# A decoder trunk on one core: token gather with a PSUM bank per feature block, ranks by tile, high halves first

## What is computed

```python
for l in range(DEPTH):
    mix = hybrid_mixer(x, positions, w_in[l], ...)       # 4 latent, 6 forgetting, 6 dilated heads
    x = layer_norm(ALPHA * x + mix, ...)
    xa = memory_cross_attention(x, mem, xattn_w_q[l], xattn_w_kv[l], xattn_w_o[l])   # 4 heads, 256 tokens
    x = layer_norm(ALPHA * x + xa, ...)
    gates = shared_group_router(x, router_w, router_bias)
    x = layer_norm(ALPHA * x + moe_ffn(x, gates, w_gate, w_up, w_down), ...)

def shared_group_router(x, router_w, router_bias):       # 16 experts in 4 groups of 4
    scores = sigmoid(x @ router_w)
    grp = (scores + router_bias).reshape(B, S, 4, 4)
    g_sel = argmax(sum of the two best of each group)
    expert_idx = two best experts inside group g_sel
    w = scores[expert_idx]; w = w / sum(w)
    return one_hot(expert_idx) * w
```

## Time and profile before

| what | value |
|---|---|
| three runs | 843.35, 837.23, 838.66 us |
| median | 838.66 us |
| the profiled execution | 841.01 us |
| its span | 839.4 us |
| mean granted clock of TensorE | 0.988 |
| memory traffic | 177 MB, 211 GB/s over the span |

### The profile page before, as it was taken

The page is one execution under the profiler, slowest core; times in us unless marked ns, Lnnn a source line. Parts: engine busy times, 40 slices in busy tenths (PEclk is TensorE's granted clock), DMA queues, the critical chain, the costliest instruction groups (busy, mean ns, idle before and its releaser), DMA issues.

```text
span 839.4 us, 12175 instructions
## 1 busy us (share of the span) xinstructions
PE 807.6 (96%) x4382; PEld 692.6 (83%) x4382; DVE 631.0 (75%) x1098; ACT 499.9 (60%) x788; POOL 87.1 (10%) x165
## 2 busy tenths in 40 slices
PE   7899999999998999999999999999999999999995
PEld 7899887789876888888899998868998768888884
DVE  4657868785558899999755686787655679999995
ACT  4755554454435788888455654645443557888872
POOL 3148100020000000000020440001000100000001
PEclk9999999999999999999999999999999899999998
DMA  9954433473334799999655543435633339999951
GB/s 284 336 180 167 138 124 127 152 241 114 126 100 126 243 369 366 366 368 377 212 156 168 203 151 109 147 131 172 204 102 124 126 102 313 364 370 364 369 198 51
DMA packets 122095, 177.06 MB, mean 211 GB/s; under 512 B 10177, under 2 KB 90577, under 8 KB 122033
## 3 DMA queue, kind: packets, MB, share of 16 engines
q1 hardware_dynamic: 120048, 169.56, 60.5%
q0 software_dynamic: 1984, 6.70, 2.9%
HBM read 175.18 MB, written 1.05 MB: 210 GB/s over the span
## 4 chain that ended last, share of the span: by engine, by line
PE 81%; DVE 9%; ACT 3%; issue 3%; DMA 2%; POOL 1%; SPq 0%; DVEq 0%; POOLq 0%; ACTq 0%
PE bank L1527 22%; PE bank L1529 22%; PE bank L1528 21%; DVE w_split L506 2%; DMA raw<-in_w_in_dram 2%; PE bank L1670 2%; PE bank L1711 2%; PE bank L1681 1%; DVE xs L1098 1%; PE bank L1702 1%; PE bank L1607 1%; PE bank L1818 1%; DVE xT_lo L1025 1%; PE bank L1659 1%; DVE xs L1146 1%
## 5 line engine op out<-in xcount | busy, mean ns | idle before, releaser
L506 DVE TENSOR_TENSOR w_split<-raw,w_split 128x1024 fp32r<-128x1024 f32 (+3 forms) x336 | 387.5, 1176 | 79.0 <-ACT w_split L501 73.5
L501 ACT ACTIVATE w_split<-raw 128x1024 fp32r<-128x1024 f32 (+3 forms) x336 | 335.7, 1010 | 108.8 <-PE bank L1529 93.9
L1527 PE MATMUL bank<-w_split,xg_hi 128*128 128x512 f32 x256 | 103.8, 406 | 0.0
L1528 PE MATMUL bank<-w_split,xg_hi 128*128 128x512 f32 x256 | 100.6, 393 | 0.0
L1529 PE MATMUL bank<-w_split,xg_lo 128*128 128x512 f32 x256 | 100.6, 393 | 0.0
L1527 PE MATMUL bank<-w_split,xT_hi 128*128 128x384 f32 (+2 forms) x224 | 78.2, 349 | 4.4 <-DVE w_split L506 3.6
L1529 PE MATMUL bank<-w_split,xT_lo 128*128 128x384 f32 (+2 forms) x224 | 76.3, 341 | 0.0
L1528 PE MATMUL bank<-w_split,xT_hi 128*128 128x384 f32 (+2 forms) x224 | 76.2, 340 | 0.0
L618 POOL TENSOR_SCALAR st<-st 128x1 f32<-128x1 f32 x12 | 5.6, 469 | 643.4 <-ACT junk_end L774 336.2
L1529 PEld LDWEIGHTS bank<-w_split,xg_lo 128*128 128x128 f32 x256 | 48.3, 189 | 11.0
L1527 PEld LDWEIGHTS bank<-w_split,xg_hi 128*128 128x128 f32 x256 | 48.5, 189 | 9.1
(11 more groups left out here) (305 smaller groups left out, 1589.7 us busy)
## 6 DMA issues: line engine op xcount, KB each, us to landing
raw<-in_expert_w_gate_dram SPq DMA_DIRECT2D x128, 256.0 KB, 5.4
raw<-in_expert_w_up_dram SPq DMA_DIRECT2D x128, 256.0 KB, 6.7
raw<-in_expert_w_down_dram SPq DMA_DIRECT2D x64, 512.0 KB, 7.3
raw<-in_xattn_w_kv_dram SPq DMA_DIRECT2D x32, 512.0 KB, 3.9
raw<-in_w_in_dram SPq DMA_DIRECT2D x40, 384.0 KB, 3.9
raw<-in_w_mix_out_dram SPq DMA_DIRECT2D x16, 512.0 KB, 3.7
raw<-in_xattn_w_q_dram SPq DMA_DIRECT2D x16, 512.0 KB, 3.5
raw<-in_xattn_w_o_dram SPq DMA_DIRECT2D x16, 512.0 KB, 5.0
```

The source lines that it names most:

```text
L501: nc.scalar.activation(w_hi[:, i % SPL, 0:w], raw[:, i % RAW, 0:w], ACT.Copy).then_inc(hi_ready, 1)
L506: nc.vector.tensor_tensor(w_lo[:, i % SPL, 0:w], raw[:, i % RAW, 0:w], w_hi[:, i % SPL, 0:w].bitcast(F32), ALU.subtract).then_inc(lo_ready, 1)
L1527: nc.tensor.matmul(o, lhs[0], rhs[0], start=first, stop=False, skip_group_check=shared)
L1528: nc.tensor.matmul(o, lhs[0], rhs[1], start=False, stop=False, skip_group_check=shared)
```

## The change

`XG_APART` goes: all eight feature blocks have a bank of their own, blocks 6 and 7 the banks 5 and 4. ScalarE makes eight `xg_hi` and VectorE eight `xg_lo`. The ranks of tile 0 and of tile 1 go to banks 4 and 5, with a signal each; the count of each group goes to bank 5 too, and is compared (`over_full`) ahead of block 6, whose first matmul waits for it. `iota` starts at 1, and the −1 step goes. In the routing two pairs of independent steps wait together. `router_first` moves from ahead of the ranks to behind the last `xg_lo`, two splits move ahead of the first `xg_lo`. The fillers become 6, 3, 11 and 2.

The logits are made by half tiles, high products first, and `XT0c`'s second low half moves behind tile 1's addition and scaling. The logits lie in pair 2. `XQ0`'s first piece is made with its high-half products first (`high_first`); `XT0b` moves to pair 3. `head_qk` of head 10 no longer waits for `s_masked`. The overflow path has a semaphore for each layer, and GpSimd's branch for the case without overflow goes.

```diff
-        ("XT0b", 2, 2, 0), ("XT1b", 2, 2, 2), ("MV1", 0, 2, 1), ("XQ0", 2, 0, 0), ("XQ1", 2, 0, 1),
-        ("XO0", 0, 2, 0), ("XO1", 0, 0, 1), ("XT0c", 2, 2, 0), ("XT1c", 2, 2, 1), ("RT", 1, 0, 0)]
+        ("XT0b", 2, 2, 3), ("XT1b", 2, 2, 2), ("MV1", 0, 2, 1), ("XQ0", 2, 0, 0), ("XQ1", 2, 0, 1),
+        ("XO0", 0, 2, 0), ("XO1", 0, 0, 1), ("XT0c", 2, 2, 0), ("XT1c", 2, 2, 1), ("RT", 1, 0, 2)]
...
-XG_BANKS = (0, 6, 7, 2, 3, 1)
-XG_APART = {6: (6, 7), 7: (2, 3)}
+XG_BANKS = (0, 6, 7, 2, 3, 1, 5, 4)
...
         more, both = (R[i][:, 0:2 * TT * NG].rearrange("p (g i) -> p g i", i=2) for i in (4, 5))
-        step(nc.vector.tensor_tensor(more, first, second, ALU.max))
-        step(nc.vector.tensor_tensor(both, first, second, ALU.add))
         across, within, score = (G4(R[i]) for i in (6, 7, 8))
-        step(nc.vector.tensor_tensor(across, more[:, :, 0], more[:, :, 1], ALU.add))
-        step(nc.vector.tensor_tensor(within, both[:, :, 0], both[:, :, 1], ALU.max))
+        step(nc.vector.tensor_tensor(more, first, second, ALU.max),
+             nc.vector.tensor_tensor(both, first, second, ALU.add))
+        step(nc.vector.tensor_tensor(across, more[:, :, 0], more[:, :, 1], ALU.add),
+             nc.vector.tensor_tensor(within, both[:, :, 0], both[:, :, 1], ALU.max))
         step(nc.vector.tensor_tensor(score, across, within, ALU.max))
...
-    def place_tokens(l):
+    def place_tokens(l, t):
         step = stepper(l)
-        dve.wait_ge(ranked.sem, ranked.at(l, 1))
-        pg = posg[:, :, :].rearrange("p t g -> p (t g)")
-        step(nc.vector.tensor_tensor(pg, bank[4][:, 0:TT * NG], ing, ALU.mult))
-        step(nc.vector.tensor_scalar(pg, pg, -1.0, None, ALU.add))
+        dve.wait_ge(ranked.sem, ranked.at(l, t + 1))
+        step(nc.vector.tensor_tensor(posg[:, t, :], bank[4 + t][:, 0:NG], ing[:, t * NG:(t + 1) * NG], ALU.mult))
...
             .then_inc(sel_ready.sem, 1)
+
+    def low_tokens(l, t):
         dve.wait_ge(xs_a.sem, xs_a.at(l, t + 1))
...
+    def over_full(l):
+        nc.vector.tensor_scalar(fl[:, 0:NG], bank[5][:, NG:2 * NG], P + 0.5, None, ALU.is_gt)\
+            .then_inc(counted_over.sem, 1)
+
     def full_group(l):
-        nc.vector.tensor_scalar(fl[:, 0:NG], bank[4][:, TT * NG:TT * NG + NG], P + 0.5, None, ALU.is_gt)\
-            .then_inc(counted_over.sem, 1)
         dve.wait_ge(counted_over.sem, counted_over.at(l, 1))
-        nc.vector.tensor_tensor(fl[:, NG:2 * NG], fl[:, 0:NG], iota[:, 0:NG], ALU.mult).then_inc(counted_over.sem, 1)
+        nc.vector.scalar_tensor_tensor(fl[:, NG:2 * NG], iota[:, 0:NG], -1.0, fl[:, 0:NG], ALU.add, ALU.mult).then_inc(counted_over.sem, 1)
         dve.wait_ge(counted_over.sem, counted_over.at(l, 2))
...
             split_lo(dve, index[l, "RT", j])
-        turn_x(l, "XT0c", 0)
+        turn_half(l, "XT0c", 0, 0)
         wait_job(l, "XO1")
...
         scale(l, 1, 1)
+        turn_half(l, "XT0c", 0, 1)
         norm_halves(l, 1, 1, x_half)
...
         router_groups(l)
-        router_first(l)
-        place_tokens(l)
+        place_tokens(l, 0)
         choose(l, 0)
+        place_tokens(l, 1)
+        over_full(l)
+        low_tokens(l, 0)
         choose(l, 1)
+        low_tokens(l, 1)
         split_lo(dve, u + 1)
-        for f in range(KC - len(XG_APART)):
+        split_lo(dve, u + 2)
+        for f in range(KC):
             dve.wait_ge(xg_a.sem, xg_a.at(l, f + 1))
...
                 .then_inc(xg_v.sem, 1)
-            if f in (1, 5):
-                split_lo(dve, u + (2 if f == 1 else 3))
+            if f == 3:
+                split_lo(dve, u + 3)
         split_lo(dve, u + 4)
+        router_first(l)
         router_gates(l)
...
+    def high_first(l, name, turned_by):
+
+        open_job(l, name)
+        w_parts = sub_in(index[l, name, 0])
+        for t_ in turned_by:
+            pe.wait_ge(job_a.sem, job_a.at(l, evac_a[job[t_]]))
+        for high in (True, False):
+            if not high:
+                for t_ in turned_by:
+                    ready(l, t_)
+            for kc in range(2):
+                for cb in range(4):
+                    o = banks(name)[cb // 2][:, (cb % 2) * T:(cb % 2 + 1) * T]
+                    hi, lo = (v[:, kc * 512 + cb * P:kc * 512 + (cb + 1) * P] for v in w_parts)
+                    if high:
+                        nc.tensor.matmul(o, hi, xT_hi[:, kc, :], start=kc == 0 and cb % 2 == 0, stop=False,
+                                         skip_group_check=True)
+                        nc.tensor.matmul(o, lo, xT_hi[:, kc, :], start=False, stop=False, skip_group_check=True)
+                    else:
+                        ins = nc.tensor.matmul(o, hi, xT_lo[:, kc, :], start=False, stop=False,
+                                               skip_group_check=True)
+        ins.then_inc(split_free, 1)
+
     def keep_busy(n):
...
         if in_pair(h):
-            pe.wait_ge(s_masked.sem, s_masked.at(l, 2 * h))
+            if in_pair(h - 1):
+                pe.wait_ge(s_masked.sem, s_masked.at(l, 2 * h))
             pe.nop().then_inc(paused_t, 1)
...
-        keep_busy(13)
+        keep_busy(11)
         pe.wait_ge(route.sem, route.at(l, group_at))
...
             for s in range(t + 1):
-                nc.tensor.matmul(bank[4][:, t * NG:(t + 1) * NG], (ones if s < t else upto)[:, :],
-                                 ing_r[:, s * NG:(s + 1) * NG], start=t == 0, stop=False, skip_group_check=True)
+                ins = nc.tensor.matmul(bank[4 + t][:, 0:NG], (ones if s < t else upto)[:, :],
+                                       ing_r[:, s * NG:(s + 1) * NG], start=s == 0, stop=s == t)
+            if t == 0:
+                ins.then_inc(ranked.sem, 1)
         for s in range(TT):
-            ins = nc.tensor.matmul(bank[4][:, TT * NG:TT * NG + NG], ones[:, :], ing_r[:, s * NG:(s + 1) * NG],
-                                   start=False, stop=s == TT - 1, skip_group_check=True)
+            ins = nc.tensor.matmul(bank[5][:, NG:2 * NG], ones[:, :], ing_r[:, s * NG:(s + 1) * NG],
+                                   start=s == 0, stop=s == TT - 1, skip_group_check=True)
         ins.then_inc(ranked.sem, 1)
-        keep_busy(5)
-        together = range(KC - len(XG_APART))
-        for t in range(TT):
-            pe.wait_ge(sel_ready.sem, sel_ready.at(l, t + 1))
-            pe.wait_ge(xs_a.sem, xs_a.at(l, t + 1))
-            for f in together:
-                nc.tensor.matmul(bank[XG_BANKS[f]][:, :], xs_hi[:, t, f * P:(f + 1) * P], sel[:, t, :],
-                                 start=t == 0, stop=False)
-            pe.wait_ge(xs_v.sem, xs_v.at(l, t + 1))
-            for f in together:
-                ins = nc.tensor.matmul(bank[XG_BANKS[f]][:, :], xs_lo[:, t, f * P:(f + 1) * P], sel[:, t, :],
-                                       start=False, stop=t == TT - 1)
-                if t == TT - 1:
-                    ins.then_inc(xg_done.sem, 1)
-        for f, apart in XG_APART.items():
-            for v, b in zip((xs_hi, xs_lo), apart):
-                pe.wait_ge(xg_v.sem, xg_v.at(l, XG_BANKS.index(b) + 1))
-                for t in range(TT):
-                    ins = nc.tensor.matmul(bank[b][:, :], v[:, t, f * P:(f + 1) * P], sel[:, t, :],
-                                           start=t == 0, stop=t == TT - 1)
-            ins.then_inc(xg_done.sem, 1)
+        keep_busy(2)
+        pe.wait_ge(sel_ready.sem, sel_ready.at(l, 1))
+        pe.wait_ge(xs_a.sem, xs_a.at(l, 1))
+        for f in range(KC):
+            if XG_BANKS[f] == 5:
+                pe.wait_ge(counted_over.sem, counted_over.at(l, 1))
+            nc.tensor.matmul(bank[XG_BANKS[f]][:, :], xs_hi[:, 0, f * P:(f + 1) * P], sel[:, 0, :],
+                             start=True, stop=False)
+        pe.wait_ge(xs_v.sem, xs_v.at(l, 1))
+        for f in range(KC):
+            nc.tensor.matmul(bank[XG_BANKS[f]][:, :], xs_lo[:, 0, f * P:(f + 1) * P], sel[:, 0, :],
+                             start=False, stop=False)
+        pe.wait_ge(sel_ready.sem, sel_ready.at(l, 2))
+        pe.wait_ge(xs_a.sem, xs_a.at(l, 2))
+        pe.wait_ge(xs_v.sem, xs_v.at(l, 2))
+        for f in range(KC):
+            nc.tensor.matmul(bank[XG_BANKS[f]][:, :], xs_hi[:, 1, f * P:(f + 1) * P], sel[:, 1, :],
+                             start=False, stop=False)
+            nc.tensor.matmul(bank[XG_BANKS[f]][:, :], xs_lo[:, 1, f * P:(f + 1) * P], sel[:, 1, :],
+                             start=False, stop=True).then_inc(xg_done.sem, 1)
...
         gemm(index[l, "MV1", 3])
-        ready(l, "XT0b")
-        ready(l, "XT1b")
-        for j in range(4):
+        high_first(l, "XQ0", ("XT0b", "XT1b"))
+        for j in range(1, 4):
             gemm(index[l, "XQ0", j])
...
-        ready(l, "XT0c")
         open_job(l, "RT")
...
-        def score_tokens(t, chunks):
+        def score_tokens(t, h, name):
+            chunks = range(4 * h, 4 * h + 4)
+            slot = index[l, "RT", h] % SPL
+            o = 2 * NE * t
```

(14 more changed lines are left out.)

49 lines of the change are left out of this document (23 added, 26 removed).

## The result

| kernel | executions | median us | range us |
|---|---|---|---|
| before | 4 | 839.50 | 837.23 to 843.35 |
| after | 4 | 823.66 | 821.90 to 826.64 |

The changed kernel takes 0.9837 of the time before (95% interval 0.9803 to 0.9870), 1.6% less. The forecast was 826.3 us, within 821.5 to 832. On two other chips its medians were 825.85 (before there: 838.91) and 825.56 (838.31), which is 13.1 and 12.8 less; the 15.8 of the table holds two executions of the changed kernel at a clock of 0.997, and none of the 40 executions of the kernel before that were taken beside the experiments reached that clock. The profiled execution took 826.64 us: a span of 825.0 at a mean granted clock of 0.993, against 839.4 at 0.988.

The account below looks back on a forecast made before the run. TensorE, busy 96% of the span, was taken as the bound. Edits of 2.3 + 2.2 + 7.6 = 12.1 us and 2.9 of clock gave 841.0 − 12.1 − 2.9 = 826.0, the median route 826.6; taken 826.3, range 821.5 to 832.

Parts of the forecast that it names:

- dilated heads: Dropped wait for the maximum at head 10; a split behind head 9's softmax is late next; 2.3 us in two layers.
- queries: First piece starts on high-half products, so TensorE no longer waits for xT_lo; 1.1 us a layer, 2.2 together.
- logits: Tile 1's addition starts some 0.45 us earlier, its high products no longer wait (some 0.35); 0.8 a layer.
- routing, two pairs: Two pairs of independent VectorE steps lose the wait between them and overlap; 0.2 us a layer.
- ranks: From ing to sel only tile 0's rank matmul and one step remain; sel comes 0.8 us earlier.
- clock: Layer 1's low-clock stretches: 1.7 us back in the gather, half of the logits' 2.4 (1.2); 2.9 in all.
- Gather: 32 matmuls without bank waits, first expert matmul 4.6 us earlier; VectorE loses 0.8, leaving 3.8 a layer, logits included.
- (d): Slower: fewer fillers and new short pauses in logits and before ranks drop the clock; 840.7 us, chance 0.04.
- (a): VectorE sets the pace in the gather, which gains only 2.0 us a layer; 829.9 us, chance 0.14.
- (b): Gains in heads and queries are handed back at the next wait; 830.8 us, chance 0.12.
- (c): Clock never falls in the two layers; 825.1 us, or 822.5 with upper bounds for logits and gather; chance 0.08.
- (e): Tile 0's rank signal is seen late, both tiles in one queue; 0.3 us a layer lost; within forecast's 0.62.

Follow-up runs that it names:

- fill_flag: Changed kernel with five more fillers a layer and full_group's three small steps moved behind the turns of experts 1 to 14: 821.60 us, 0.9812 of before.
- changed_again: The changed kernel run once more, unaltered, beside other experiments: 825.85 us, 0.9839 of the time before.
- fill_none: Changed kernel without the 22 filler matmuls a layer in logits, routing and ranks: 831.82 us, 0.9898 of the time before.
- fill_gaps: Changed kernel with five more filler matmuls a layer in the logits and ahead of the ranks: 823.73 us, 0.9822 of before; run again, 823.39 us.
- heads_wait: Changed kernel with head 10's wait for s_masked put back: 830.29 us, 0.990 of the time before.
- rotate_later: fill_flag with GpSimd's rotation of the dilated queries also waiting for head 1's norm: 822.63 us, 0.9831 of the time before.

## Why the prediction was right

The time came within 2.6 us of the median forecast, and the sum was made of the right parts. A check without the traces' stages: at a granted clock of 0.993 the kernel before took 837.0 us on average (11 executions) and the changed one 825.3 (3), 11.7 less, where the edits alone were forecast at 12.1 and come to 11.8 in the table (14.4 less the clock's 2.55). In the two profiled executions:

| term | forecast | measured |
|---|---|---|
| dilated heads, two layers | 2.3 | 1.19 + 1.20 = 2.4 |
| queries, two layers | 2.2 | 1.07 + 1.01 = 2.1 |
| logits, a layer | 0.8 | 0.77 |
| routing, two pairs, a layer | 0.2 | 0.24 |
| ranks, a layer | 0.8 | 0.74 |
| banks, a layer | 2.8 | 2.71 |
| handed back to VectorE, a layer | −0.8 | −0.4 |
| from `XO1` to the transpose, a layer | 3.8 | 4.06 |
| clock | 2.9 | 2.55 |
| not forecast | 0 | −0.8 |
| sum | 15.0 | 14.4 |

**Dilated heads.** Right, with the new wait in the place named.

**Queries and logits.** Right. The mechanism of the logits was seen only in half: that half of `xT_lo` would fill the wait of VectorE for GpSimd's `st` was not in the text, but its 0.45 was.

**Routing.** The Trainium skill, "VectorE: DVE Perf Modes", section "The DRAIN you can't avoid", measured that dropping the waits in a row of eight copies gained nothing. It adds that a next operation which isn't held starts earlier. Dropping the waits here did gain: the two steps of a pair start 0.09 us apart (254.32 and 254.41) where chained ones start some 0.20 apart, and with the waits put back the stretch goes from 2.62 to 2.87 us. The edit there was one of independent steps, which a chain is not.

**Gather.** The bound on TensorE was right (7.40 us for 7.3). VectorE's part was mis-sized: I had it late at the sixth `xg_lo` by 0.3 and at the activation by the rest of 0.8. Counted from the first gather matmul, I had the sixth `xg_lo` at 269.9 − 259.55 = 10.35 and it came at 266.23 + 1.29 − 257.43 = 10.1. The wait came where it was forecast, at the third piece, but cost 0.1 and not 0.3. Some 0.1 more was lost up to the gates' end and 0.24 at the activation, 0.4 in all and not 0.8. fill_flag shows that 0.23 of this was three small steps in the wrong place. `sel` to the first expert's matmul took 8.14 us, a little over the 7 to 8 that was to show the mechanism.

**Clock.** The size was right in these two traces: layer 1's gather gave back 1.5 us (1.7 forecast) and its logits 1.0 (1.2). Part of it is luck of one execution. Of the changed kernel's three profiles one has a low stretch of 3.4 us in this stage, one has none (span 822.5 us), and changed_again has one of 13.7, more than the kernel before had in its profile. What stays true is what fill_none and fill_gaps bracket: the granted clock is 0.977 without fillers and 0.996 with the waits covered. The Trainium skill, "TensorE: Matmul & The Clock Gate", Part 1, calls the low clock the default that activity releases; these two runs agree with it.

**Rival (d)** was right in kind and not in reach: short pauses do cost the clock, in some executions, at 1.4 us for a stretch of 3.4 (32.85 against 31.47) and 5.1 for one of 13.7 (36.56 against 31.47). My argument against it, that pauses of 1.48 us stay at full clock, failed: heads_wait has the same pause with the clock at 0.66. **Rivals (a) and (b)** fall: VectorE is late twice, by 0.1 and 0.24 us, and only 0.7 us was handed back. **(c)** is what some executions are: 821.90 and 822.51 us. **(e)** costs little: VectorE waits 0.43 for tile 0's ranks and `sel` still comes 0.74 earlier.

**What the sum had no term for** is −0.15 ahead of the heads, which is less than the scatter there (below), and −0.68 at head 1 of layer 1. rotate_later shows the cause of the second: there TensorE's lead moved VectorE's norm into another phase of GpSimd's rotation. Before, the same two steps took 0.43 and 1.02 us and TensorE didn't wait. The −0.06 of the last row is the next expert's: 8.52 us, where it was 8.47.

**The scatter that is left at one clock**, 821.90 to 824.11 us at 0.997, can be read from the traces. The changed kernel's three profiles reach the first dilated head at 114.92, 111.45 and 113.80 us. From there to the last matmul they take 700.05, 703.68 and 698.65 us, and without what their low stretches cost (1.38, 5.09 and 0) 698.67, 698.59 and 698.65. So beside the clock's stretches in the layers these profiles differ only ahead of the dilated heads, and there first in one wait for a weight split. Timeline of the changed kernel, then of fill_gaps:

```profile
33.67 0.41 PE L1534 MATMUL bank<-w_split,xT_hi 128*128 128x384 f32 x1 [2.33 <-DVE w_split L505]
...
32.20 0.41 PE L1534 MATMUL bank<-w_split,xT_hi 128*128 128x384 f32 x1 [0.88 <-DVE w_split L505]
```

In 8 of the 14 profiles this wait is 2.0 to 2.4 us long, and in 7 of the 8 the clock falls right behind it for 3.4 us. In the other six it is 0.9 or less, and the clock stays up. The first matmul of head scores comes at 62.5 to 63.7 us in the eight and at 60.1 to 60.8 in the six. Why the wait is long in one execution and short in another was not tried, nor was a filler put there.

## What to carry to other kernels

Give a consumer its own bank before giving it a cleverer order: the four waits for a borrowed bank cost more than all reordering of the routing. When a wait goes, look for what was finished just behind it, since that is the new bound (here a split 1.2 us behind), and move every small step that nobody waits for behind the ones that somebody does. Behind each short pause of TensorE put work that costs nothing, and compare kernels at the same granted clock and from a matmul behind the start.
